# The end of a Strassen-type MLP and the final norm: squares and roots of four rows at once, and ScalarE's order of weight and hidden roundings

## The reference

```python
    h = h + merged @ w_out[l]
    z = rmsnorm(h, norm_mlp[l])
    h = h + jnp.square(jax.nn.relu(z @ w_up[l])) @ w_down[l]   # w_up 1024 x 4096
    return rmsnorm(h, norm_final)                              # x * rsqrt(mean(x*x) + 1e-6) * g
```

## Time and profile before

| | |
|---|---|
| median of 3 runs (lowest, highest) | 1497.07 us (1497.02, 1497.55) |
| the profiled execution | 1496.87 us |
| its span in the profile | 1494.8 us |
| mean granted TensorE clock | 0.995 |
| busy: PE, DVE, ACT, POOL | 98%, 66%, 35%, 35% |
| last matmul of the program ends | about 17 us before the end |

### The profile page before, as it was taken

How to read it: one execution, slowest core, us unless ns; L and a number is a source line. 1 busy time by engine, 2 the same in 40 slices (tenths; PEclk the granted TensorE clock), 3 DMA queues, 4 the chain that set the end, 5 groups by cost and what they waited for, 6 DMA issues and landing times.

```text
span 1494.8 us, 20639 instructions
## 1 busy us (share of the span) xinstructions
PE 1465.8 (98%) x7019; PEld 1210.5 (81%) x7019; DVE 981.0 (66%) x1911; ACT 517.9 (35%) x1003; POOL 519.2 (35%) x349
## 2 busy tenths in 40 slices
PE   9999999999999999999999999999999999999995
PEld 8887888888888888888888888878787878787874
DVE  6898564543467527675624788595958586767678
ACT  7422312400122212241101322545444444444455
POOL 4000001245332332004333003273737373646556
PEclk9999999999999999999999999999999999999998
DMA  7225543282111101003542001333333333333333
GB/s 221 99 90 143 144 109 124 72 279 88 57 43 43 43 29 57 29 29 131 179 176 71 1 29 50 120 99 116 103 112 106 104 108 107 108 107 110 107 111 135
DMA packets 150933, 149.02 MB, mean 100 GB/s; under 512 B 19104, under 2 KB 109904, under 8 KB 150864
## 3 DMA queue, kind: packets, MB, share of 16 engines
q1 hardware_dynamic: 118048, 107.00, 23.2%
q10 hardware_dynamic: 32816, 41.12, 8.5%
HBM read 126.58 MB, written 21.50 MB: 99 GB/s over the span
## 4 chain that ended last, share of the span: by engine, by line
PE 84%; DVE 9%; issue 3%; ACT 2%; POOL 1%; ACTq 1%; DMA 0%; DVEq 0%; POOLq 0%
PE acc L799 19%; PE acc L801 19%; PE acc L800 19%; PE aux L800 7%; PE aux L801 7%; PE aux L799 7%; DVE h_ring L2602 1%; DVE h_res L2634 1%; PE aux L1081 1%; PE aux L1074 1%; PE aux L1084 1%; DVE h_sum L2609 1%; PE aux L964 1%; PE aux L958 0%; PE aux L1069 0%
## 5 line engine op out<-in xcount | busy, mean ns | idle before, releaser
L799 PE MATMUL acc<-z_hi,w_hi 128*128 128x512 f32 x448 | 177.2, 396 | 0.6 <-DVE z_lo L1874 0.6
L801 PE MATMUL acc<-z_hi,w_lo 128*128 128x512 f32 x448 | 174.6, 390 | 0.0
L800 PE MATMUL acc<-z_lo,w_hi 128*128 128x512 f32 x448 | 174.5, 390 | 0.0
L799 PE MATMUL acc<-w_hi,z_hi 128*128 128x512 f32 x384 | 164.4, 428 | 0.0
L801 PE MATMUL acc<-w_hi,z_lo 128*128 128x512 f32 x384 | 150.5, 392 | 0.0
L800 PE MATMUL acc<-w_lo,z_hi 128*128 128x512 f32 x384 | 149.6, 390 | 0.0
L663 POOL CAST w_hi<-stage 128x1024 fp32r<-128x1024 f32 x22 | 27.7, 1259 | 344.2 <-PE acc L801 290.0
L650 POOL TENSOR_SCALAR stage<-stage,nm 128x512 f32<-128x512 f32 x48 | 78.3, 1643 | 168.8 <-PE acc L801 86.0
L767 POOL TENSOR_TENSOR t_raw<-t_raw,p_a 128x512 f32<-128x512 f32 x28 | 39.5, 1409 | 262.3 <-DMA p_a<-in_w_up 157.1
L799 PEld LDWEIGHTS acc<-z_hi,w_hi 128*128 128x128 f32 x448 | 84.1, 188 | 19.8 <-issue 1.5
L801 PEld LDWEIGHTS acc<-z_hi,w_lo 128*128 128x128 f32 x448 | 84.1, 188 | 17.9
(11 more groups left out here) (417 smaller groups left out, 3879.7 us busy)
## 6 DMA issues: line engine op xcount, KB each, us to landing
stage<-in_w_in SPq DMA_DIRECT2D x28, 512.0 KB, 4.4
p_a<-in_w_up SPq DMA_DIRECT2D x56, 256.0 KB, 2.8
p_a<-in_w_down SPq DMA_DIRECT2D x56, 256.0 KB, 2.6
gate_dram<-gate_t ACTq DMA_DIRECT2D x32, 256.0 KB, 2.1
p_b<-in_w_up SPq DMA_DIRECT2D x28, 256.0 KB, 2.7
p_b<-in_w_down SPq DMA_DIRECT2D x28, 256.0 KB, 2.7
x_in<-in_x SPq DMA_DIRECT2D x8, 512.0 KB, 6.1
stage<-in_w_in SPq DMA_DIRECT2D x32, 128.0 KB, 2.3
```

The lines of the kernel that those rows point to most:

```text
L799: nc.tensor.matmul(out, s_hi, m_hi_, start=first, stop=False, skip_group_check=partial)
L800: nc.tensor.matmul(out, s_hi, m_lo_, start=False, stop=False, skip_group_check=partial)
L801: return nc.tensor.matmul(out, s_lo, m_hi_, start=False, stop=last, skip_group_check=partial)
```

## The change

Three edits in the lists, with no change to what is computed:

1. In every turn, from step 15 on, ScalarE rounds the weight pieces of a step ahead of its hidden tile instead of behind it.
2. In the last turn, ScalarE squares rows 4 and 5 ahead of its rounding of hidden tile 12, row 6 behind it, row 7 behind tile 13. GpSimd's product of a row with nf, which waits for a row's square, can follow from there. The left halves of rows 0 to 3 are squared after m = 5 and multiplied by GpSimd as halves; their right halves are squared after `add_row` and finished by VectorE (four instructions of line 2749 of the changed kernel).
3. Roots are made for four rows at once: 128x4 instructions, TENSOR_SCALAR for three and TENSOR_TENSOR or SCALAR_TENSOR_TENSOR with both inputs in SBUF for nine. There are two such roots instead of four pairs. Stores go out as four rows and eight halves instead of seven rows and two halves.

The diff, cut to its core:

```diff
@@ ScalarE, win_block: a turn's list (edits 1 and 2)
                 for s in range(PIECES):
                     if s == 8:
                         hidden_hi(0)
+                    if s >= 15:
+                        cast_pieces(s, g, more)
+                    if s == 24 and not more:
+                        square_f(0)
+                        square_f(1)
+                    if s == 25 and not more:
+                        square_f(2)
                     if 15 <= s <= 25:
                         hidden_hi(s - 12)
+                    if s == 25 and not more:
+                        square_f(3)
...
-                    cast_pieces(s, g, more)
+                    if s < 15:
+                        cast_pieces(s, g, more)
@@ ScalarE, the end
+            for i in range(4):
+                square_left(i)
+            square_right(0)
             scale_f(0)
+            square_right(1)
             scale_f(1)
-            square_f(4)
-            square_f(5)
+            square_right(2)
+            square_right(3)
             scale_f(2)
             scale_f(3)
...
@@ GpSimd
+            for p in range(4):
                 pool.wait_ge(f_ss, p + 1)
-                nc.gpsimd.tensor_tensor(h_res[:, c, :], h_res[:, c, :], nf[:], ALU.mult).then_inc(f_done_pool, 1)
+                nc.gpsimd.tensor_tensor(h_res[:, 4 + p, :], h_res[:, 4 + p, :], nf[:], ALU.mult).then_inc(f_done_pool, 1)
+            for i in range(4):
+                pool.wait_ge(f_half, i + 1)
+                nc.gpsimd.tensor_tensor(h_res[:, i, 0:HALF], h_res[:, i, 0:HALF], nf[:, 0:HALF], ALU.mult)\
+                  .then_inc(f_done_pool, 1)
@@ VectorE, last_rows: one root step, and the order
+                    V.tensor_tensor(prod_t, guess, guess, ALU.mult).then_inc(f_level, 1)
+                    level(u, 4 + 3 * step)
+                    V.tensor_tensor(prod_t, prod_t, mean, ALU.mult).then_inc(f_level, 1)
+                    level(u, 5 + 3 * step)
+                    V.scalar_tensor_tensor(out=rs2[:, 4 * u:4 * u + 4] if step == 2 else guess, in0=prod_t, scalar=1.5,
...
+                add_pair(5, 0)
+                dve.wait_ge(f_ss, 4)
+                V.tensor_scalar(mean, ss2[:, 0:4], -0.5 / D, -0.5 * EPS, ALU.mult, ALU.add).then_inc(f_level, 1)
+                root_guess(0)
                 add_pair(5, 1)
-                root_means(0)
-                root_rest(0)
+                root_step(0, 0)
+                root_step(0, 1)
                 add_row(0)
+                root_step(0, 2)
+                add_row(1)
...
```

More of the change, by code:

```diff
@@ L1841, in square_half @@
[L1841 to L1850, removed]
+                act.wait_ge(f_rstd, 1)
@@ L2634, in add_pair @@
                     V.tensor_tensor(rows, rows, (acc, aux)[m % 2][:, 2 * b:2 * b + 2, :], ALU.add).then_inc(out_free, 1)
-                for s in range(26 if last else PIECES):
+                for s in range(25 if last else PIECES):
                     for b in range(2):
@@ L2675, in add_row @@
                     V.tensor_tensor(h_res[:, j, hs], h_res[:, j, hs], acc[:, j, :], ALU.add).then_inc(out_free, 1)
[L2677 to L2681, removed]
+                bits, mean, guess, prod_t, left = [rs_bits[:, 0:4]] + [rs_tmp[:, k, 0:4] for k in range(4)]
                 def level(u, n):
-                    dve.wait_ge(f_level, 8 * u + n)
@@ L2693, in root_guess @@
                     level(u, 2)
[L2694 to L2702, removed]
@@ L2730, in last_rows @@
-                root_rest(1)
-                add_row(2)
-                dve.wait_ge(f_rstd, 2)
-                root_means(2)
-                add_row(3)
-                root_rest(2)
-                dve.wait_ge(f_rstd, 3)
-                a, b = both(ss2, 3)
-                dve.wait_ge(f_ss, NCH - 1)
-                V.tensor_scalar(mean[0], a, -0.5 / D, -0.5 * EPS, ALU.mult, ALU.add)
-                dve.wait_ge(f_half, 1)
-                V.tensor_scalar(half, half, -0.5 / D, -0.5 * EPS, ALU.mult, ALU.add).then_inc(f_half, 1)
@@ new lines, in last_rows @@
+                add_row(1)
+                dve.wait_ge(f_half, 4)
+                V.tensor_scalar(left, left, -0.5 / D, -0.5 * EPS, ALU.mult, ALU.add).then_inc(f_level, 1)
+                add_row(2)
+                add_row(3)
+                dve.wait_ge(f_rstd, 1)
+                dve.wait_ge(f_ss, NCH)
+                level(0, 12)
+                V.scalar_tensor_tensor(out=mean, in0=ss2[:, 4:8], scalar=-0.5 / D, in1=left, op0=ALU.mult, op1=ALU.add)\
+                 .then_inc(f_level, 1)
@@ L2759, in _ @@
+                root_guess(1)
+                for step in range(3):
+                    root_step(1, step)
+                dve.wait_ge(f_rstd, 2)
+                dve.wait_ge(nf_in, 16)
+                for i in range(4):
+                    V.scalar_tensor_tensor(out=h_res[:, i, HALF:D], in0=h_res[:, i, HALF:D], scalar=rs2[:, 4 + i:5 + i],
+                                           in1=nf[:, HALF:D], op0=ALU.mult, op1=ALU.mult).then_inc(f_done, 1)
             for f in range(N_PLAIN):
```

109 lines of the change are left out of this document (47 added, 62 removed).

## The result

| | before | changed |
|---|---|---|
| median (lowest, highest), 5 runs each | 1497.25 us (1497.02, 1497.55) | 1521.64 us (1518.68, 1521.70) |
| the profiled execution, its span | 1496.87, 1494.8 us | 1521.66, 1519.9 us |
| last matmul of the program ends | 1477.69 us | 1502.40 us |

The ratio is 1.0156 (95% interval 1.0142 to 1.0170): 24.4 us slower. The forecast was 1517.0, and the median lies 0.6 us above the upper end of its range. Three runs are at 1521.6 to 1521.7, two at 1518.7 and 1519.1.

A forecast was written before the change was run, and what follows sets the result against it. VectorE's list was taken as the bound once a turn, and the chain of squares, roots, scalings and stores behind the last matmul. 13.6 for the turns plus 6.3 for the end made 19.9, so 1517.0 us; range 1509 to 1521.

The forecast's parts named there:

- What bounds the kernel: Before step (2, 0) of each turn: VectorE's instruction list is the bound, with a TensorE stall of 1.0 us.
- The hold: VectorE instructions with two SBUF inputs and GpSimd's work exclude each other; the later asker starts 0.14 before the other's end.
- Edit 1, 1.94 a turn: GpSimd's earlier split of piece 18 delays VectorE, so step (2, 0) starts 1.94 us later; seven turns, +13.6.
- Edit 2, 4.8: End of last turn: GpSimd's earlier products hold VectorE's work on tiles 12 and 13; m = 6 starts 4.8 us later.
- the first race: Last turn: VectorE's tile 12 instruction asks 0.09 us before GpSimd's first product; 0.7 more if GpSimd won.
- Edit 3: 128x4 root instructions wait for GpSimd products; whole end +6.6 us, m = 6's delay 4.8 of it, taken as +6.3.
- The clock: The 4.8 us stand before m = 6 may halve TensorE's clock for 24 matmuls, costing nearly nothing.
- Small operations pass: Rival for the first root: 128x4 operations aren't held, the end costs 2.0; 1512.6 us, chance 0.22.
- Weights were the bound: Rival: the turns' stall is GpSimd's t_b split, rounding first saves 7.1 us, the end 2.1; 1488, chance 0.05.
- the turns don't care: Rival: VectorE's delays are caught up before step (2, 0), only the end pays +6.3; 1503 us, chance 0.08.
- all hidden: Rival: no hold in the turns and only the end's small gain; 1495 to 1500 us, chance 0.03.
- the clock never fell in a turn: Judges the rival that stalls bring TensorE's clock down, another 2.7 us each turn; about 1536, chance 0.07.

The follow-up runs named there:

- e9: Kernel before, with VectorE's split of hidden tile 4 moved ahead of the two adds of m = 0: 1489.13 us, ratio 0.9937.
- e8: Kernel before with ScalarE's weights-first order, but GpSimd's split of piece 18 waits until VectorE has split hidden tile 3: 1503.80 us, ratio 1.0039.
- e11: Kernel before with only the last turn's squares moved ahead among the last roundings; roots, halves and stores as before: 1502.48 us, ratio 1.0029.
- e12: Changed kernel, all edits kept, with VectorE's split of hidden tile 4 moved ahead of the two adds of m = 0: 1505.28 us.
- e1: Kernel before with only the weights-first rounding, from step 15 on in all turns, its end as before: 1512.30 us, ratio 1.0098.
- e10: Changed kernel with the old turns and all four whole-row squares behind the rounding of hidden tile 13; new roots, halves, stores kept: 1506.18 us, ratio 1.0052.
- e2: Kernel before with weights-first rounding at step 15 only, that is weight piece 18: 1510.53 us, ratio 1.0084.

## Where the prediction was right, and where not

- **What bounds the kernel** was right. VectorE's list is the bound once a turn: moving one instruction in it takes the stall away and nothing else appears (e9). Two of seven rows named GpSimd's split of t_b as the releaser; those stalls went in e9 too, with no change on GpSimd.
- **The hold**, with its 0.14, was right. In the changed kernel s1 takes 1.68 and split 3 1.77; the working gave 1.67 and 1.74. With split 18 held back they are at 0.69 again (e8).
- **Edit 1, 1.94 a turn** was right for the place it was worked out at: 1.9 to 2.0, with both stalls: step (1, 1) starts 1.2 and step (2, 0) 1.7 to 1.9 later than in a dense row. The step that failed is the sentence behind it, "I find no third stall", and the sum 7 x 1.94 = 13.6. There is one more of 0.3 in each of six turns, at tile 13, where a sum of GpSimd holds the split by 0.25. It stood in the text as the upper bound ("2.4 if one more hold falls on tile 13's split at a turn's end"), and I left it out of the sum. 13.6 + 6 x 0.3 = 15.4; measured 15.4.
- **Edit 2, 4.8** was right: 4.82. The rounding of 12 ends at 1487.25, split 12 at 1489.09, s4 for tile 13 at 1491.85, split 13 at 1494.61: less the 18.1 of the turns 1469.15, 1470.99, 1473.75 and 1476.51, against 1470.98, 1473.75 and 1476.52 in the text for the last three. VectorE won the first race by 0.05.
- **Edit 3** was right in its kind: 128x4 instructions are held, whichever operation they are. On the old clock the second add of m = 5 ends at 1482.4 (1482.4 in the text), `add_row(3)` at 1488.0 (1488.4), the second root starts at 1490.5 (1490.8). Worked +6.6, taken +6.3, measured 7.0. The mis-sized step is the cut from 6.6 to 6.3 for stores that overlap better, and what follows the last `add_row`: 13.8 to the end of the span, where the text has 13.0 (1488.4 to 1501.4). The adds ended 0.4 earlier than worked out, and what follows them took 0.8 longer.
- **The clock** fell as it might, and at the price said. It was at half not for all 24 matmuls, as the text has it, but for the first nine of m = 6, so the last matmul is 1.8 later than its stand alone makes it, and nothing came of it: `add_row(0)` had to wait for a held root step that ended at 1502.62, 0.2 after the last matmul. In e11 the last matmul ends 7.2 later by the stand and the clock together, and the span ends 4.8 later, which is the stand alone.
- **What was missing altogether** is the 2.6 us before the turns, in a stretch that no edit touches. It is not a price of the change: e12 holds all three edits and enters its first turn 0.2 late (see the last section). Without it the profiled execution would be at 1519.1, where the two lowest runs are.
- **The rivals.** "Small operations pass" fell with the 1.20s above. "Weights were the bound" fell with e1 and e9, "the turns don't care" with e1, "all hidden" with the measured time, and the clock never fell in a turn, though two stalls stand there, 4.6 us apart from start to start.

The total is then 15.4 + 7.0 + 2.6 = 25.0, against 13.6 + 6.3 = 19.9.

## What to carry to other kernels

Where two engines exclude each other, a job that is done earlier than anyone needs it can be the dearest change: ask whose instructions stand in the time it moves into. Before blaming the engine that a stall names, look whether the list ahead of its last instruction holds work that nobody waits for yet; moving one split ahead of one add was worth 8.5 us here (medians of e9 and its before). And when a bound is written down with its mechanism ("if one more hold falls on ..."), follow the list to that place before leaving it out of the sum.

## What the runs showed that I had not expected

**DMA issues on ScalarE vary from run to run.** At 120 us ScalarE issues eight DMAs of y_dram ahead of an activation that TensorE waits for. PE's wait for it, in the kernel before, the changed kernel and e9:

```profile
PE aux L947 <- ACT abt L1483: 1.0, 1, 1.0
```

```profile
PE aux L953 <- ACT abt L1489: 2.0, 1, 2.0
```

```profile
PE aux L947 <- ACT abt L1483: 2.9, 1, 2.9
```

The timeline of ScalarE (119.5 to 123.5 us) has the issues, before and then changed:

```profile
119.93 3.58 ACTq L1471 DMA_DIRECT2D y_dram<-y_blk  x7
```

```profile
119.99 3.58 ACTq L1477 DMA_DIRECT2D y_dram<-y_blk  x5
```

The same 3.58 us hold seven issues or five. In each of the 13 profiled executions exactly one of the eight is long, from 0.72 to 2.62 us, and the others take 0.34 to 0.51; it is 0.79 before, 1.74 in the changed kernel and 2.62 in e9. In the two executions with waits of 2.0 and 2.9 TensorE's clock then stood at half for 3.3 us, as in this window of the changed kernel, which has 1.00 in the kernel before:

```profile
140.30:143.60 3.30, 3.30 (x20) 2.58 (x17) 1.87 (x4) 0.13 (x1) 0.00 (x0) 0.50 0.88 274
```

That makes 1.0 + 1.6 us in the changed kernel and 1.8 + 1.6 in e9. Three others (e10, e2, e11) waited 1.7 to 1.9 and kept the clock. It fits the two groups of the changed kernel's runs and e9's spread of 3.9 us, but only profiled executions show it; why an issue takes longer stays open.

**A 128x4 instruction with a single SBUF input is held too.** TENSOR_SCALAR reads one tensor, and took 1.20 beside half products and 2.3 beside whole ones; in 128x1 form it passed, 0.32 for four. The Trainium skill ("SBUF — State Buffer", section "Who interferes with whom") has tensor_scalar among the operations that can enter a mode with two ports and contend with GpSimd, and "VectorE: DVE Perf Modes" (section "Mode 2×_2P") has that mode split a tensor along a dimension of more than one element, which a single column lacks. The traces agree with both.
